# Scaling the compressed branch on VectorE, with earlier selection stages, no bias on the diagonal tile and the last transposes behind the first output block

## What is computed

```python
a = rmsnorm(x)                                  # one input projection gives u, q, three K/V pairs, gates
# compressed branch: 127 block keys
p_cmp = softmax(where(blk_end <= t, q @ kcmp.T * SCALE, -1e30))
o_cmp = p_cmp @ vcmp
# selection: importance of 32 blocks of 64 keys, the 16 best of each query;
# block 0, the query's own block and the one before it are always taken
imp = where(j > cur, -inf, where(forced, inf, p_cmp.sum(heads) @ overlap))
sel = top_k(imp, 16)
o_sel = softmax(q @ k[sel].T * SCALE, causal) @ v[sel]
o_win = softmax(q @ k[last 512].T * SCALE) @ v[last 512]
y_nsa = g0 * o_cmp + g1 * o_sel + g2 * o_win    # g: sigmoid gates
h = x + concat([pool_mixer(u), y_nsa]) @ w_out
h = h + swiglu(rmsnorm(h)); h = h + (p @ w_ple_proj) * sigmoid(rmsnorm(h) @ w_ple_gate)
out = rmsnorm(h)
```

## Time and profile before

| | us |
|---|---|
| median of 3 runs (lowest, highest) | 1831.11 (1830.16, 1831.39) |
| profiled execution, its own time | 1834.28 |
| its span, slowest core (all cores) | 1832.7 (1827.6 to 1832.7) |
| TensorE matmul busy | 1683.1 (92%) |
| VectorE busy | 559.6 (31%) |
| ScalarE busy | 426.9 (23%) |
| GpSimd busy | 278.2 (15%) |

### The profile page before, as it was taken

One profiled execution on the slowest core, in us unless ns is written; L12 is line 12 of the kernel. 1 busy time (PEld: TensorE's weight loads), 2 busy tenths in 40 slices (PEclk: granted clock), 3 DMA queues, 4 the chain that ended last, 5 costly groups with the idle time before them and its releaser, 6 DMA issues.

```text
span 1832.7 us, 25154 instructions; the slowest of 8 cores (1827.6 to 1832.7 us)
## 1 busy us (share of the span) xinstructions
PE 1683.1 (92%) x9006; PEld 829.3 (45%) x9006; DVE 559.6 (31%) x1322; ACT 426.9 (23%) x739; POOL 278.2 (15%) x339
## 2 busy tenths in 40 slices
PE   4699998788877899999999999999999999999994
PEld 1344544556554444444444444444444444444443
DVE  3553343443444212511022011310112210135546
ACT  4452212555546512100000000000000000123232
POOL 3332000012330033100000000000000000054321
PEclk8799999899999999999999999999999999999997
DMA  8675402011109810654029350584502934335414
GB/s 203 153 169 87 72 15 47 2 24 24 47 1 150 169 61 1 105 102 81 12 39 166 71 92 1 91 152 80 92 1 50 166 69 84 63 58 81 75 45 141
DMA packets 31322, 144.00 MB, mean 79 GB/s; under 512 B 4576, under 2 KB 9184, under 8 KB 22240
## 3 DMA queue, kind: packets, MB, share of 16 engines
q0 software_dynamic: 16416, 108.04, 35.4%
q1 hardware_dynamic: 14784, 34.35, 5.8%
HBM read 242.03 MB, written 8.39 MB: 137 GB/s over the span
## 4 chain that ended last, share of the span: by engine, by line
PE 84%; DVE 6%; issue 3%; ACT 3%; DMA 2%; POOL 1%; DVEq 0%; ACTq 0%; SPq 0%; POOLq 0%
PE ps L1195 17%; PE ps L1172 16%; PE ps L1169 16%; PE ps L513 12%; PE ps L1148 6%; PE ps L1273 4%; PE ps L854 3%; PE ps L723 2%; PE ps L739 2%; DMA arena<-xin 1%; DVE arena L1121 1%; PE ps L726 1%; DMA arena<-wup 1%; DVE arena L702 1%; ACT arena L798 1%
## 5 line engine op out<-in xcount | busy, mean ns | idle before, releaser
L1169 PE MATMUL ps<-arena 128*128 128x512 bf16 x1408 | 319.5, 379 | 2.0 <-DVE arena L1121 2.0
L1172 PE MATMUL ps<-arena 128*128 128x512 bf16 x1408 | 318.3, 379 | 0.9 <-DMA arena<-wup 0.9
L1195 PE MATMUL ps<-arena 128*128 128x512 bf16 x1408 | 306.6, 380 | 0.0
L1176 ACT ACTIVATE arena<-ps 128x512 f32<-128x512 f32 x88 | 52.7, 598 | 781.3 <-PE ps L1169 773.7
L1177 DVE TENSOR_TENSOR arena<-ps,arena 128x512 bf16<-128x512 f32 x88 | 60.9, 692 | 539.4 <-PE ps L1169 311.4
L513 PE MATMUL ps<-arena 128*128 128x512 bf16 x960 | 220.4, 387 | 0.1
L1169 PEld LDWEIGHTS ps<-arena 128*128 128x128 bf16 x1408 | 137.7, 98 | 169.7 <-issue 4.9
L1195 PEld LDWEIGHTS ps<-arena 128*128 128x128 bf16 x1408 | 138.2, 98 | 167.5 <-issue 2.8
L1172 PEld LDWEIGHTS ps<-arena 128*128 128x128 bf16 x1408 | 137.7, 98 | 167.2 <-issue 1.4
L1075 DVE TENSOR_TENSOR arena<-ps,arena 128x512 f32<-128x512 f32 x160 | 110.7, 692 | 281.2 <-PE ps L1195 204.0
L1087 POOL TENSOR_TENSOR arena<-arena 128x512 f32<-128x512 f32 (+2 forms) x98 | 115.4, 1177 | 244.2 <-ACT arena L1086 231.7
(11 more groups left out here) (144 smaller groups left out, 1133.6 us busy)
## 6 DMA issues: line engine op xcount, KB each, us to landing
arena<-wdown POOLq DMA_DIRECT2D x16, 1536.0 KB, 14.6
arena<-wgate POOLq DMA_DIRECT2D x22, 1024.0 KB, 10.6
arena<-wup POOLq DMA_DIRECT2D x22, 1024.0 KB, 12.6
arena<-xin SPq DMA_DIRECT2D x32, 512.0 KB, 4.8
arena<-wB POOLq DMA_DIRECT2D x20, 512.0 KB, 14.3
arena<-xT SPq DMA_DIRECT2D x16, 512.0 KB, 9.4
arena<-wout POOLq DMA_DIRECT2D x4, 2048.0 KB, 35.8
arena<-wpg POOLq DMA_DIRECT2D x4, 2048.0 KB, 23.3
```

What stands on the lines that cost most here:

```text
L1169: PE(lambda e, dc=dc: e.matmul(ps[pg][:], lhsT=wgu[sl][:, dc, half * 128:(half + 1) * 128], rhs=a2T[t][:, dc, :], start=(dc == 0), stop=(d ...
L1172: PE(lambda e, dc=dc: e.matmul(ps[pu][:], lhsT=wgu[sl + 1][:, dc, half * 128:(half + 1) * 128], rhs=a2T[t][:, dc, :], start=(dc == 0), sto ...
L1195: PE(lambda e, ci=ci: e.matmul(ps[pb][:], lhsT=wt_[:, ci, mm * 128:(mm + 1) * 128], rhs=hT[:, ci, t * 512:(t + 1) * 512], start=(ci == 0), ...
```

## The change

- The four scalings of s1b go from ScalarE (`activation` with Copy) to VectorE (`tensor_scalar`).
- The stages stand at steps 0, 2, 2, 3 and ntot - 5 instead of 0, 2, 3, 4 and ntot - 2. So s1b follows s1 in the same step; the hold that s1 sets is 4 instead of 3.
- The diagonal tile of the selected branch gets no selection bias (eight matmuls of L726 fewer). The blocks in that tile are the query's own one, the one before it, or later ones, which the causal mask of the same tile takes out.
- The last chain's transposes are not emitted at the pipeline's end but behind the first block of the output projection, and so are the last four residual loads, which take the place of that chain's buffers.

```diff
         def s1():
             close_fill()
-            fstate["hold"] = 3
+            fstate["hold"] = 4
...
             for r in (3, 0, 1, 2):
                 bank, c0 = bankof(r)
-                ACT(lambda e, bank=bank, c0=c0, r=r: e.activation(out=oa[:, r, :], in_=ps[bank][:, c0:c0 + 128], func=AF.Copy, scale=r_[:, 2, r:r + 1]), [PB[bank], Br], [B_oa])
+                DVE(lambda e, bank=bank, c0=c0, r=r: e.tensor_scalar(out=oa[:, r, :], in0=ps[bank][:, c0:c0 + 128], scalar1=r_[:, 2, r:r + 1], scalar2=None, op0=ALU.mult), [PB[bank], Br], [B_oa])
...
-                at.setdefault((0, 2, 3, 4, ntot - 2)[k], []).append(f)
+                at.setdefault((0, 2, 2, 3, ntot - 5)[k], []).append(f)
...
-                        pi = score_exp(kall[:, row, kt * 128:(kt + 1) * 128], [B_kk[row][kt]], g, ot, bias=kt if br == 1 and ot >= 4 else None,
+                        pi = score_exp(kall[:, row, kt * 128:(kt + 1) * 128], [B_kk[row][kt]], g, ot, bias=kt if br == 1 and ot >= 4 and kt < ltq else None,
...
-    while deferred:
-        deferred.pop(0)[1]()
+    last_tr = [d[1] for d in deferred]
+    assert len(last_tr) == 1
...
-    for m in range(16):
-        S.inherit(B_h[m], old_of[m])
-    for m in xord:
-        S.dma("sp", lambda e, m=m: e.dma_start(out=hres[m].rearrange("p a b -> p (a b)"), in_=xT_d[m]), f"hres{m}", [], B_h[m])
+    def load_h(ms):
+        for m in ms:
+            S.inherit(B_h[m], old_of[m])
+            S.dma("sp", lambda e, m=m: e.dma_start(out=hres[m].rearrange("p a b -> p (a b)"), in_=xT_d[m]), f"hres{m}", [], B_h[m])
+    load_h(xord[:12])
+
+    def end_attention():
+        last_tr[0]()
+        load_h(xord[12:])
...
-    run_blocks(blocks, {24: ...
+    run_blocks(blocks, {0: [end_attention], 24: ...
```

More of the change, by code:

```diff
@@ L1156, in build @@
     blocks = [d_block(q, mm, t) for (q, t) in quarter_order() for mm in range(4)]
-    run_blocks(blocks, {24: [lambda: norm_sum(0)], 26: [lambda: norm_scale(0, 0, lambda m: a2T[0][:, m, :], lambda m: B_a2T[0][m])]}, 4)
+    run_blocks(blocks, {0: [end_attention], 24: [lambda: norm_sum(0)], 26: [lambda: norm_scale(0, 0, lambda m: a2T[0][:, m, :], lambda m: B_a2T[0][m])]}, 4)
     flush()
```

## The result

The changed kernel takes 1863.45 us (median of 4 runs, 1863.01 to 1864.42), the kernel before 1831.25 us (median of 4): a ratio of 1.0178, 95% interval 1.0165 to 1.0191. It is slower by 32.2 us, where 6.8 were predicted, and outside the range of 1822 to 1848. The profiled execution took 1863.01 us, its span is 1861.5.

The account below looks back on a forecast made before the run. It took the attention pipeline as bound by TensorE's waits, mainly score matmuls behind exp; 17.4 - 7.0 - 1.8 - 3.3 - 1.0 - 6.0 + 8.5 = +6.8 us on 1831.1 gave 1837.9 us, range 1822 to 1848.

Parts of the forecast that it names:

- part 1: Attention pipeline: scalings on VectorE remove 34.8 us of waits for exp, add 52.2 at transposes L709: +17.4 us.
- Parts 2 and 4: Earlier selection stages end L726's wait for L810, -7.0 us; first output block fills the gap before the last transposes, -3.3.
- Part 3: Selected branch's diagonal tile: eight bias matmuls fewer at 0.22 us each, -1.8 us.
- Part 5: Fill queue of pooling work: fewer units closed before s1, less of L779's wait behind L862, -1.0 us (0 to -4).
- Part 6: Granted clock: -6.0 us from three low stretches gone, +8.5 (0 to 10) from 13 of 14 waits low instead of eight.
- The clock does not follow: Rival, 24%: the six pipeline gaps that kept the full clock keep it; 1829.4 us, no change.
- ScalarE's relief wins: Rival, 20%: new waits at L709 no longer than the old gaps, no new low clock; faster, 1812.6 us.
- VectorE's queue is longer than shown: Rival, 9%: pooling instructions waiting for POOL ahead of s1 delay the evacuation too; slower still, 1847 us.
- Does not free the first step: Rival, 3%: negT is late for a chain's second step; the 7.0 us and 4.4 of clock stay, 1849 us.

Follow-up runs that it names:

- a3: The changed kernel with the transposes of a chain's result deferred three steps more (7 instead of 4): 1814.18 us, ratio 0.9906 to the kernel before.
- b3: The kernel before with only s3 earlier, no bias on the diagonal tile, and last transposes and loads behind the first output block: 1819.20 us.
- b2: The kernel before with only the hold set to 4 steps instead of 3: 1841.10 us, ratio 1.0048.
- d2: The changed kernel with the fill queue saving a credit of at most 2 pieces instead of 4: 1853.10 us.
- a1: The changed kernel with the four scalings of s1b on ScalarE again: 1845.05 us.
- c1: The changed kernel with the hold of 3 again instead of 4: 1836.87 us.
- a4: The changed kernel with 188 matmuls whose results nobody reads added in front of the transposes L709: 1841.12 us.
- d1: The changed kernel with hold 3 and the transposes deferred by 7 instead of 4: 1807.74 us.

## Why the prediction was right or wrong, point by point

- **Direction, and part 1: right.** L709's new waits were put at 52.2 and measured 54.0 us; the eight with a selection average 35.2 / 8 = 4.4, put at 4.2 (they lie between 4.2 and 4.8). The other six average 3.1, put at 3.1, but lie between about 1 and 5.4: there the agreement is luck. The scaling on VectorE takes 350 ns, put at 351 by L702's row. a3 shows the cause: given three steps more, L709 waits 4.3.

  The Trainium skill, "VectorE: DVE Perf Modes", section "The TRN2 errata", led to an estimate of 258 ns for it; the row of 350 disagrees, and the measurement decides.
- **Parts 2 and 4: right** to a tenth in their waits (b3). That s3 costs nothing where it now stands held too: no wait at L809 shows up. Part 3 was not measured by itself.
- **Part 5 failed.** The step said that fewer forced closings would take some of L779's wait, -1.0 (0 to -4); the waits that it stands for rose by 14.6. By the same count forced closings do fall, from six to three, but L779 waits for L862 ten times instead of five. The step counted closings and the loads of wo; it did not count how closely pieces follow one another. The hold by itself costs 7.1 us at the pieces and 1.3 at L779 (b2), and with a credit of 2 most of the pieces' wait goes (d2). That is 8.4 of the 14.6 us. The 2.3 of L779 behind L710 in the rows above belong to the hold too: b2 has 1.8, a1 2.2 and d2 2.3 of it, and no run with a hold of 3 has any. Of the other 6 us, 5.0 are L739's waits, 2.6 of them one event behind L702; no run took them apart, and they stay open.
- **Part 1's sentence on the hold was true, and not priced.** It said that a hold of 4 leaves no pooling matmuls in step 5 to fill the wait. c1 gives the price, 18.9 us at L709 and the pieces together (7.2 of them bunching, by b2). It is part of the 54.0, so the term came out right; but the hold was the change's most expensive number, and nothing in the prediction says so. That c1's 1836.87 lies near the forecast of 1837.9 is no support for it: the terms there are others (L709 25.3, pieces 21.8).
- **Part 6 failed in its size, not in its mechanism.** It expected a low clock behind 13 of 14 stands, and it is behind 13: in the seven microseconds behind each (the rows in the section on the result show three) the granted clock is 0.57 to 0.80. But 1.7 us a stand was the loss behind the stands of before, where 0.76 is the common row, (1 - 0.76) x 7 = 1.7. After, the thirteen lose 1.4 to 3.0, 29.4 in sum, 2.26 each, and one behind L779 loses 2.1 more; the ten of before that lie inside the pipeline lose 17.3. That is 14.2 us more, near the 13.1 of the ledger. Of the 6.0 us credited to parts 2 and 4 the 1.6 at the end came; of the other 4.4, b3 got 1.9, since other stands took the low rows over (13 of them against 15).
- **The rivals.** "The clock does not follow" and "ScalarE's relief wins" fell with the clock row of 0.88 and the 54.0 us. "VectorE's queue is longer than shown" would have shown as more than 52 us at L709; it is within 2; the time lies above that rival's 1847 for other reasons. "Does not free the first step": L726 waits 0.
- **The range** failed since both failing terms were bounded by too little: 0 to -4 for the queue and 0 to 10 for the clock. No row of before has a hold of another length, so the first bound had nothing under it, and an increase was not allowed for at all; the second was made from the common rows, though the trace had a dearer one, behind the 3.40 us of L726 (0.50 in the earlier trace rows, 2.5 us).

Three rows of the kernel before on which the account of part 6 rests: the common one, the dearest (as far as the next stand), and the one behind the shortest stand that cost anything, 1.41 us.

```profile
439.82:446.82 7.00, 6.95 (x45) 4.51 (x46) 2.78 (x12) 2.95 (x7) 0.03 (x1) 0.76 0.16 32
555.07:561.24 6.17, 6.17 (x34) 3.61 (x34) 1.89 (x10) 2.46 (x5) 0.00 (x0) 0.59 1.03 170
607.86:614.86 7.00, 6.08 (x39) 3.43 (x40) 2.06 (x8) 3.59 (x6) 0.00 (x0) 0.76 1.02 157
```

## What to carry to other kernels

A number that only spaces out filler work (a hold, a credit, a deferral) is an edit of its own: count, step by step, in front of which waiting instruction a piece stood before and after, and how often two pieces that share a buffer follow directly on each other. When work moves onto a queue ahead of a result that is waited for, move the reader too; the same reordering that lost 32 us gained 17 with the reader three steps later, and 29 with the filler set right as well. Price a stand of TensorE by the low clock behind it too, with the dearest row in the trace as the upper bound and not the common one: 13 x 2.5 = 32.5 us would have covered the 29.4 measured.

## What the runs showed of the hardware

Work added to TensorE made the kernel faster: 188 matmuls of 0.22 us in the stands took 22 us off the time, with a granted clock of 0.98 instead of 0.88 over the pipeline (a4). How long a stand is doesn't by itself say what follows it: in the kernel before the row stayed at 1.00 behind 2.43 us and fell to 0.76 behind 1.41 us (607.86 above). Behind two stands of 4.2 us after (595.04 and 633.22 above) the seven microseconds were granted 0.77 and 0.57. The same stand of the same chain, 2.44 us long in the kernel before (439.82 above) and 2.49 us in b3, was followed by seven microseconds at 0.76 in the one and at 1.00 in the other. Nor does the sum of waits say it: 47.3 us in a3 came with ten low rows, 49.0 us in d1 with five. What else decides it, no run here took apart.
